# RWKV chunk stage: T from the transpose of its transpose, operands laid out by head parity, two blocks in step

## The reference, cut to what matters

```python
def step(state, inp):
    w_t, kk_t, kka_t, k_t, v_t, r_t = inp
    sk = jnp.einsum('dbhvk,dbhk->dbhv', state, kk_t)
    new = (state * w_t[..., None, :] - sk[..., :, None] * kka_t[..., None, :]
           + v_t[..., :, None] * k_t[..., None, :])
    y_fwd = jnp.einsum('bhvk,bhk->bhv', new[0], r_t[0])
    y_bwd = jnp.einsum('bhvk,bhk->bhv', state[1], r_t[1])
    return new, jnp.stack([y_fwd, y_bwd])
...
y = ys[:, 0] + jnp.flip(ys[:, 1], axis=0)
```

## Time and profile before

| | us |
|---|---|
| median of 3 runs | 3633.68 (3628.63 to 3635.43) |
| the profiled execution | 3633.06, its span 3631.3 |
| TensorE busy | 3480.8 (96% of the span) |
| VectorE busy | 1845.9 (51%) |
| ScalarE busy | 1182.9 (33%) |
| GpSimd busy | 667.7 (18%) |
| chunk stage of the first layer | from 711 us |
| chunk stage of the second layer | from 1916 us |

### The profile page before, as it was taken

How to read it: one execution, slowest core, us unless ns; L and a number is a source line. 1 busy time by engine, 2 the same in 40 slices (tenths; PEclk the granted TensorE clock), 3 DMA queues, 4 the chain that set the end, 5 groups by cost and what they waited for, 6 DMA issues and landing times. The chain is left out here.

```text
span 3631.3 us, 52208 instructions
## 1 busy us (share of the span) xinstructions
PE 3480.8 (96%) x22144; PEld 2769.1 (76%) x22144; DVE 1845.9 (51%) x2604; ACT 1182.9 (33%) x1641; POOL 667.7 (18%) x460
## 2 busy tenths in 40 slices
PE   7999998989999999999898899999899999989999
PEld 6888774586888788887548788887678887768887
DVE  6777636735455567664575543345543335373332
ACT  3222333524222322223352432233442223253223
POOL 4202111131202120211014121220011211001112
PEclk9999999999999999999999999999999999999999
DMA  6565421002444355442000222323032322122331
GB/s 210 179 195 171 129 72 35 7 27 83 124 148 125 113 166 188 152 155 82 31 13 27 71 89 92 101 83 93 24 105 93 101 96 85 59 70 93 96 101 58
DMA packets 445211, 357.99 MB, mean 99 GB/s; under 512 B 15990, under 2 KB 441012, under 8 KB 444980
## 3 DMA queue, kind: packets, MB, share of 16 engines
q1 hardware_dynamic: 444980, 354.67, 31.1%
HBM read 350.43 MB, written 2.10 MB: 97 GB/s over the span
## 5 line engine op out<-in xcount | busy, mean ns | idle before, releaser
L587 DVE TENSOR_TENSOR ring_wlo<-ring_raw,ring_whi 128x2048 fp32r<-128x2048 f32 (+3 forms) x268 | 570.9, 2130 | 376.6 <-ACT ring_whi L568 346.5
L568 ACT ACTIVATE ring_whi<-ring_raw 128x2048 fp32r<-128x2048 f32 (+3 forms) x278 | 490.4, 1765 | 652.0 <-PE f_ps L1076 242.9
L1074 PE MATMUL f_ps<-act_hi,ring_whi 128*128 128x512 f32 x1280 | 502.0, 392 | 3.3 <-DVEq L1228 3.3
L1076 PE MATMUL f_ps<-act_hi,ring_wlo 128*128 128x512 f32 x1280 | 498.7, 390 | 0.0
L1075 PE MATMUL f_ps<-act_lo,ring_whi 128*128 128x512 f32 x1280 | 498.1, 389 | 0.0
L1184 POOL TENSOR_TENSOR f_glo<-f_v,f_ghi 128x512 fp32r<-128x512 f32 x88 | 238.0, 2704 | 1030.2 <-ACT f_ghi L1176 1030.2
L1074 PEld LDWEIGHTS f_ps<-act_hi,ring_whi 128*128 128x128 f32 x1280 | 240.3, 188 | 53.6 <-DVEq L1228 5.0
L1166 ACT ACTIVATE f_t<-f_ps 128x512 f32<-128x512 f32 x88 | 52.6, 598 | 695.6 <-PE f_ps L1076 648.2
L1076 PEld LDWEIGHTS f_ps<-act_hi,ring_wlo 128*128 128x128 f32 x1280 | 240.2, 188 | 50.7
L1075 PEld LDWEIGHTS f_ps<-act_lo,ring_whi 128*128 128x128 f32 x1280 | 240.4, 188 | 49.0
L1074 PE MATMUL f_ps<-f_ghi,ring_whi 128*128 128x512 f32 x704 | 277.0, 393 | 0.0
(11 more groups left out here) (598 smaller groups left out, 6014.2 us busy)
## 6 DMA issues: line engine op xcount, KB each, us to landing
ring_raw<-in_w_ff_in SPq DMA_DIRECT2D x176, 512.0 KB, 4.8
f_ada_raw<-in_w_ada SPq DMA_DIRECT2D x128, 512.0 KB, 5.3
ring_raw<-in_w_mlp SPq DMA_DIRECT2D x64, 1024.0 KB, 5.1
ring_raw<-in_w_in SPq DMA_DIRECT2D x42, 1024.0 KB, 5.1
ring_raw<-in_w_ff_out SPq DMA_DIRECT2D x32, 768.0 KB, 4.5
ring_raw<-in_w_ff_out SPq DMA_DIRECT2D x32, 640.0 KB, 4.0
ring_raw<-in_w_out SPq DMA_DIRECT2D x16, 1024.0 KB, 5.5
ada_raw<-in_w_ada SPq DMA_DIRECT2D x16, 512.0 KB, 8.5
```

The source lines that it names most:

```text
L568: eng.activation(self.w_hi[:, i % self.SPLIT, 0:s.nk, 0:w], self.raw[:, i % self.RAW, 0:s.nk, 0:w], ACT.Copy)\
L587: eng.tensor_tensor(self.w_lo[:, i % self.SPLIT, 0:s.nk, 0:w], self.raw[:, i % self.RAW, 0:s.nk, 0:w], self.w_hi[:, i % self.SPLIT, 0:s.nk ...
L1074: eng.matmul(out, wh, o_hi[:, a, :], start=(s.first and q == 0), stop=False)
L1076: return eng.matmul(out, wl, o_hi[:, a, :], start=False, stop=(s.last and q == s.nk - 1))
```

## The change

All of it lies in the chunk stage but for one mask.

- X is no longer computed. Only T^T is updated (`second` makes XT alone), and after each level, as at the start, T is the transpose of T^T by TensorE (`inverse_turned`, entry "TN", four transposes of 128x128), copied by ScalarE to T0. This swaps heads and chunks on the partitions: the rows of T0 are by head parity, its columns by chunk.
- `first` therefore multiplies with rows by head parity, in all four quadrants, into two banks; ScalarE copies each half of Z apart. MB is made from MA, the masked M part of MR with rows by parity. VectorE writes MA in four operations on 64 partitions each (`masked`), two of which change the partition half.
- `mirrored` and the product M are gone; VectorE makes the start of T^T from MR (`started`), with the other direction's mask in `k.pairs`. GpSimd no longer works on T.
- The R part of MR goes to ME (`kept`), which also holds Bt beside it, so that `moved` is one product of 128 columns in place of two of 64.
- GpSimd sums the two directions of NR's R part (`summed`); `ended` uses the sum: three products a head in place of four.
- `moved` for blocks 0 and 1 stands in level 2 of pair 2, `solved` in level 1, `ended` in levels 3 and 4; AT, BT, KT of block 0 stand ahead of level 1. Within a level the order is Z, Z, work beside, XT, XT, work beside, TN, TN.
- A counter `m_read` is added for banks read out of `second`'s order.

```diff
-                added(k.pairs[:, d, :], k.between[:, 0, :], k.seen[:, 1 - d, 0:64], ALU.mult)
+                added(k.pairs[:, d, :], k.between[:, 0, :], k.seen[:, d, 0:64], ALU.mult)
...
+            def inverse_turned(b, lv):
+
+                if lv == 0:
+                    eng.wait_ge(t_first, b + 1)
+                else:
+                    read(eng, "XT", b, lv)
+                out = begin("TN", b, lv)
+                for d in (0, 1):
+                    for hh in (0, 1):
+                        col = (2 * d + hh) * P
+                        mm = eng.transpose(out[:, col:col + P], T1[b][:, d, hh, :, :].rearrange("p q c -> p (q c)"), k.ident)
                 mm.then_inc(pe_done, 1)
...
+                read(eng, "TN", b, lv - 1)
+                outs = [begin("Z", b, 2 * lv + par) for par in (0, 1)]
...
+                        for c in (0, 1):
+                            for par in (0, 1):
+                                mm = eng.matmul(outs[par][tok(c), col:col + 64], MB[i][tok(par), (lv + b // 2) % 2, d, hh, c, :],
+                                                T0[i][tok(par), d, hh, c, :], start=True, stop=True)
...
-                if lv < LEVELS:
-                    out = begin("X", b, lv)
...
+                for d in (0, 1):
+                    for hh in (0, 1):
+                        col = (2 * d + hh) * P
+                        for c in (0, 1):
+                            for par in (0, 1):
+                                mm = eng.matmul(outs[c][tok(par), col:col + P], AG[i][tok(c), d, 2 * hh + par, 0:64],
+                                                ME[b][tok(c), d, hh, par, :, :].rearrange("p n c -> p (n c)"),
+                                                start=True, stop=True)
...
+                eng.wait_ge(n_summed, b + 1)
...
+                    for n in range(3):
...
+            cross("MR", 0)
+            cross("MR", 1)
+            for name in ("AT", "BT", "KT"):
+                turned(name, 0)
+            inverse_turned(0, 0)
+            cross("NR", 0)
+            inverse_turned(1, 0)
...
+            def summed(b):
+                read(eng, "NR", b, 1)
+                eng.tensor_tensor(NR[b][:, 0, :, 1, :], NR[b][:, 0, :, 1, :], NR[b][:, 1, :, 1, :], ALU.add).then_inc(n_summed, 1)
...
+            def inverse_turned(b, lv):
+                made(eng, "TN", b, lv)
+                if lv == 0 and b >= 2:
+                    made(eng, "Z", b - 2, 2 * LEVELS + 1)
+                eng.activation(T0[b % 2][:, :, :, :, :].rearrange("p d h n c -> p (d h n c)"), bank("TN", b, lv)[:, :], ACT.Copy)\
+                   .then_inc(s_read, 1)
...
+            def masked(b):
+
                 for par in (0, 1):
...
+                    made(eng, "MR", b, par)
+                    for c in (0, 1):
+                        ins = eng.tensor_tensor(MA[b][tok(par), :, :, c, :], parts(bank("MR", b, par)[tok(c), :], 0),
+                                                k.unseen[tok(c), :, 0:64].unsqueeze(2).to_broadcast([64, 2, 2, 64]), ALU.mult)
+                ins.then_inc(a_masked, 1)
...
+            for b in (0, 1):
+                masked(b)
+                started(b)
+                kept(b)
+            later(0)
+            for a in (0, 2):
+                for lv in range(1, LEVELS + 1):
+                    if a == 0 and lv in (3, 4):
+                        masked(lv - 1)
+                    second(a, lv)
+                    if a == 0 and lv in (1, 5):
+                        later(1 if lv == 1 else 3)
+                    elif a == 0 and lv in (3, 4):
+                        started(lv - 1)
+                        kept(lv - 1)
+                    elif a == 2 and lv == 2:
+                        moved(0)
+                    second(a + 1, lv)
+                    if a == 0 and lv == 4:
+                        later(2)
+                    elif a == 2 and lv == 2:
+                        moved(1)
+            for b in (2, 3):
+                moved(b)
```

More of the change, by code:

```diff
@@ L2190, in cross, with one @@
     def cross(name, b):
[L2191 to L2200, removed]
+        order.extend([(name, b, 0, "m"), (name, b, 1, "m")])
+    def one(name, b, i=0):
+        order.append((name, b, i, "s"))
@@ L2209, in rwkv_plan @@
[L2209 to L2215, removed]
@@ L2216, in rwkv_plan @@
[L2216 to L2221 removed]
+        order.extend([("YQ", b, 0, "s"), ("YQ", b, 1, "s")])
+    cross("MR", 0)
+    cross("MR", 1)
+    for name in ("AT", "BT", "KT"):
+        one(name, 0)
+    one("TN", 0)
+    cross("NR", 0)
+    one("TN", 1)
+    for a in (0, 2):
+        for lv in range(1, LEVELS + 1):
+            first(a, lv)
+            first(a + 1, lv)
+            if a == 0 and lv in (1, 5):
+                cross("NR", 1 if lv == 1 else 3)
+            elif a == 0 and lv == 2:
+                one("AT", 1)
+                one("BT", 1)
+            elif a == 0:
+                cross("MR", lv - 1)
+            elif lv == 1:
+                solved(0)
+            elif lv == 2:
+                cross("RW", 0)
+            elif lv < 5:
+                ended(lv - 3)
+            else:
+                one("AT", 3)
+                one("BT", 3)
+            second(a, lv)
+            second(a + 1, lv)
+            if a == 0 and lv in (1, 3):
+                one("G", lv // 2)
+            elif a == 0 and lv == 2:
+                one("KT", 1)
+            elif a == 0 and lv == 4:
+                cross("NR", 2)
+            elif a == 2 and lv == 1:
+                solved(1)
+            elif a == 2 and lv == 2:
+                cross("RW", 1)
+            elif a == 2 and lv == 3:
+                one("AT", 2)
+                one("BT", 2)
+            elif a == 2:
+                one("KT", lv - 2)
+                one("G", lv - 2)
+            for b in (a, a + 1):
+                if lv < LEVELS:
+                    one("TN", b, lv)
+                elif a == 0:
+                    one("TN", b + 2, 0)
@@ L2222, in rwkv_plan @@
+    for b in (2, 3):
+        solved(b)
+    for b in (2, 3):
+        cross("RW", b)
+        ended(b)
+    place, reads = {}, {"v": 0, "s": 0, "m": 0}
     for n, (name, b, i, reader) in enumerate(order):
@@ L2446, in _ @@
-            for b in (0, 1):
-                solved(b)
-                mirrored(b + 2)
-            for lv in range(1, LEVELS + 1):
-                first(2, lv)
-                first(3, lv)
-                if lv <= 2:
-                    moved(lv - 1)
-                elif lv < LEVELS:
-                    turned("AT", lv - 1)
-                    turned("BT", lv - 1)
-                second(2, lv)
-                second(3, lv)
-                if lv <= 2:
-                    ended(lv - 1)
-                elif lv < LEVELS:
-                    turned("KT", lv - 1)
-                    guess(lv - 1)
```

376 lines of the change are left out of this document (187 added, 189 removed).

## The result

| | before | changed |
|---|---|---|
| median, us | 3632.22 (3628.63 to 3635.43, 4 runs) | 3612.64 (3608.85 to 3615.28, 4 runs) |
| ratio, 95% interval | | 0.9946 (0.9928 to 0.9963) |
| profiled execution, span | 3631.3 | 3613.6 |
| first stage, first matmul to end of last | 107.5 | 96.2 |
| second stage | 104.8 | 98.5 |

What follows compares the result with a forecast made beforehand. The stage was taken as bound by TensorE's own list: passes, seams and instruction supply. Walked groups and waits 88.1, seams 3 and stalls 4.5 gave 95.6 us a stage, 21.0 us less for both: 3612 us, range 3597 to 3626.

Steps and rivals of the forecast that it cites:

- waits for VectorE: Pair 0, levels 3 and 4: TensorE idles about 2.4 us each before a transposition, until VectorE's subtraction.
- supply stalls: TensorE out of instructions in the middle of like matmuls: four stalls of about 1.1, 4.5 us a stage, bounds 0 and 9.
- groups and seams: TensorE's stage work: 90.4 us of groups before, 17.4 less by the change, plus 3 us of seams the prices lack.
- Groups and their prices: Chunk stage, prices per TensorE group: 4.35 us less a block, 17.4 us a stage; 624 matmul records for 812.
- The beginning: Stage start: VectorE's work delays the first Z to 9.5 us, where it stood at 5.1; 2.9 us lost net.
- Levels: Pair 0: 6.7, 6.3, 8.2, 8.6, 5.6 us; pair 2: 7.75, 6.3, 7.5, 7.65, 5.45; end 8.6.
- stalls stayed at 8 or more: Sign that the prediction is wrong: supply stalls per stage staying at 8 us or more.
- Rival B: Instructions never run short in the stage: 91.1 us a stage, 3603 us, or 3597 with seams gone; chance 0.17.
- The clock: TensorE's granted clock in the stage: forecast to stay at 1.0.
- Rival D: TensorE's clock falls inside the stage after idle stretches, making the kernel slower; 25 us low in each stage give 3637; chance 0.05.
- rival A: The forecast itself: both stages 8 to 14 us shorter, 3605 to 3617 us; chance 0.55.
- rival C: New chain and supply add instead of overlapping: about 101 to 103 us a stage, 3618 to 3629 us; chance 0.19.

Runs made afterwards that it cites:

- again: The changed kernel unaltered, timed and profiled a second time: ratio to the kernel before 0.9951, stages 100.8 and 95.7 us.
- again5: The changed kernel unaltered, timed and profiled a third time: ratio to the kernel before 0.9954, stages 98.2 and 95.1 us.
- twice: Changed kernel with each of a stage's 20 transposition groups issued twice into the same bank: 3623.82 us, one run; stages sum to 206.2 us.
- rate: Changed kernel with 256 records added at each stage's end, 64x64 in layer one, 64x128 in layer two: 3633.57 us, one run.
- fill: Changed kernel with MR of block 1 multiplied twice and NR of block 0 three times, 96 records more in the beginning: ratio to the kernel before 0.9944.
- standards: Three profiles of the unaltered changed kernel, the first and two repeats: both stages sum to 193.3 to 196.4 us, mean 194.8.
- filled runs: Three runs with MR of block 1 multiplied twice and NR of block 0 three times, two with further edits: ratios to the kernel before 0.9944, 0.9943, 0.9956.
- apart: Changed kernel with `moved` undone to two products of 64 columns, 32 records more a block: 3621.03 us, one run; stages sum to 200.9 us.

## Why the prediction was right

The direction, the size and the main mechanism were right: fewer TensorE groups, a chain that shows as waits for VectorE, and supply stalls that stay. The closeness of the number was not earned term by term. Two second stages, of again and again5, have no low clock; again5's beside before's:

```profile
1906.30:2001.41 95.11, 79.56 (x2496) 72.32 (x2496) 39.62 (x80) 40.41 (x97) 33.75 (x28) 1.00 0.08 26
```

```profile
1916.24:2021.03 104.79, 93.95 (x3248) 90.42 (x3248) 47.38 (x80) 28.94 (x57) 41.82 (x32) 1.00 0.08 24
```

Such a stage lasts 95.1 us, and 95.6 was forecast. But the forecast's groups and seams were 76.0 us (90.4 - 17.4 + 3) and TensorE is busy for 79.6; its waits were 15.1 (88.1 less 73.0 of groups) and the waits are 9.8; its supply stalls 4.5, and they are 5.7.

- *Groups and their prices.* 17.4 us a stage less was the core. Single groups cost what the nearest rows said (Z in four quadrants 0.69 with tail, two transpositions 1.04, the 128-column `moved` 0.9). In all, TensorE's busy time fell by 14.4 us at full clock (93.95 to 79.56): from start to start, idle time left out, the 20 transpositions take 11.6 us for the 10.2 priced and the 20 groups of Z 11.7 for 9.4, part of which may be waits too short to show behind a tail. The page "TensorEngine Tiling (Array Packing)" of the Trainium skill says in "Key Properties" that a change of tiling mode drains the array. The 1.04 holds whatever that costs; `twice` adds transposes but no change of mode and says nothing of it.
- *The beginning.* 9.5 forecast, 10.0 measured. The shape that no row had, 64 partitions by 256, took 0.42 for one and 1.73 for four, the upper end of its bounds, where I took 0.35: 1.73 for my 1.4, twice.
- *Levels.* First stage, forecast and measured: 6.7, 6.3, 8.2, 8.6, 5.6 and 6.5, 6.6, 8.8, 8.2, 5.6 for pair 0; 7.75, 6.3, 7.5, 7.65 and 8.1, 6.4, 8.6, 11.7 for the first four levels of pair 2; 14.05 and 15.8 for the fifth and the end, which took up to 20.6 in again. VectorE's waits in levels 3 and 4 came where they were expected, but 0.98 and 1.10 us in the first stage, behind a supply stall of 1.41, and 1.67 and 1.69 in the second, not 2.4.
- *Supply.* Right as a mechanism (rate, fill), too small as a number: 6.2 and 4.4 us in the first profile, 6.7 on average in the standards for 4.5. The prediction called itself wrong if stalls stayed at 8 or more a stage, and two of the six standard stages have 9.3 and 8.2; against 16.3 for both stages before, the standards have 10.6 to 15.5. So supply gave 1 to 6 us of the gain. The fourth level of pair 2, with 2.21 us of stall, is the worst place of the first profile. Rival B, no stalls at all, fell, and with B the page "Runtime: NRT & Kernel Launch" of the Trainium skill ("Instruction fetch mechanics"), which calls the cost of crossing a 16 KB block mostly hidden: in this stage it is not, 3.4 to 3.8 us a packet bind wherever 256 instructions are worth less.
- *The clock.* My sum had it at full speed, and 17 us over both stages of the first profile stood at 1.2 GHz (3.4 in the first, 6.8 + 3.4 + 3.4 in the second). At 0.25 to 0.35 us lost per us at the low level, as level 1 shows, that is 4 to 6 us; TensorE's busy time there is 5.9 us over twice the 79.7 of stages without it. **Rival D was a real mechanism with a small price**: I gave it only the role of turning the gain into a loss, and said that a drop in the beginning would cost next to nothing. It costs 1.0 or 2.4 us, for it reaches into level 1. The page "TensorE: Matmul & The Clock Gate", Part 1, of the Trainium skill has the rule that activity releases the clock; the filled runs agree with it.
- *The sum of the first profile.* 21.0 us less was forecast for both stages and 17.6 found, 3.5 more than 191.2. Groups and seams cost 7.4 more than priced, the clock 5.9 and supply 1.6; the waits cost 11.4 less. **Errors of 14.9 and 11.4 us all but cancelled.**
- *The share of luck.* To that comes the spread: first stages of one and the same list differ by up to 4.6 us between executions. That the median lies within 1 us of 3612 is mostly chance; that the gain is clear of noise and the time in the range of rival A, 3605 to 3617, is what the mechanism earned. The bounds of rival C are looser than its own sum (101 to 103 a stage give 3623 to 3628, not 3618 to 3629), which changes no verdict.

That the beginning's stretch of low clock follows from its idle time rests on 11 of 20 against 0 of 6, which would come by chance about once in 50 if the filling did nothing. That the later ones follow from idle times was not tested; they only stand at them. What decides the length of a stall at record 2059, from 1.7 to 3.7 us, stays open, with the load of w_out the first suspect. No run undoes the main part, the X products and Z's four quadrants, by itself; its worth is read from TensorE's busy time and from the groups' prices.

## What to carry to other kernels

Price a rewrite of small matmuls by records and by quadrants used, then ask separately how many instructions it issues: here one edit that saved half a packet of instructions was worth more than its array time (apart, one profile). Fewer, wider records won twice. Where a change puts idle time into a stage that had none, add the clock to the sum as a cost of its own. When a forecast hits, compare its terms and not only its total. And look at which engine's queue the odd one of two blocks in step stands in.

## What the runs showed of the hardware

- 128 records of 64x64 in four quadrants and their weight loads, 1.87 us of array time, take 3.7 to 4.0 us in a row, as long as records twice as wide, and the instruction queue brings one 16 KB packet every 3.4 to 3.8 us meanwhile. TensorE goes on 2.4 to 3.0 us behind the beginning of the packet's column.
- Such stalls keep to the same instructions of the list in every execution; work moved by 96 or 64 records met them elsewhere, work moved by 128 or 256 at the same records. They end 2.2 to 2.9 us behind the start of an instruction packet.
- At 1.2 GHz in place of 2.4 this mix of small groups and waits lost 1.0 us in 3.4 us and 2.4 us in 6.8.
- VectorE needs 0.42 us for 64 partitions by 256 columns out of PSUM, as for 128 partitions (0.41): half the partitions cost the whole.
